# Two passes of a scan stage re-ordered: sums loaded by GpSimd, silu of the gate between differences and exponents, the inner norm's root ahead of splits

## The reference, cut to what matters

```python
cs = cumsum(dt * a)                                  # per head and chunk
lmat = exp(where(causal, cs[l] - cs[s], -inf))       # decay between two tokens of a chunk
cb = einsum('bclgn,bcsgn->bcgls', C, B)
y_diag = einsum('bcgls,bcgrls,bcsgrp->bclgrp', cb, lmat, x * dt)
states = einsum('bclgn,bclgr,bclgrp->bcgrpn', B, exp(cs[-1] - cs), x * dt)
# scan over chunks: h = exp(cs[-1]) * h + states
y_off = einsum('bclgn,bcgrpn,bclgr->bclgrp', C, h_before, exp(cs))
g = (y_diag + y_off + d * x) * silu(z)
out = (g * rsqrt(mean(g * g over the group) + 1e-6) * w) @ w_ssd_branch
```

## Time and profile before

| | |
|---|---|
| median of three runs | 2505.2 us |
| the profiled execution | 2507.65 us |
| its span, first to last instruction | 2505.8 us |
| mean granted clock | 0.989 |
| TensorE matmuls busy | 2414.6 us, 96% |
| VectorE busy | 1546.3 us, 62% |
| ScalarE busy | 873.8 us, 35% |
| GpSimd busy | 60.2 us, 2% |
| round 13, pass 1, first transposes | 1413.99 |
| second half of tile 21, pass 1, start | 1500.43 |

### The profile page before, as it was taken

The page is one execution under the profiler, slowest core; times in us unless marked ns, Lnnn a source line. Parts: engine busy times, 40 slices in busy tenths (PEclk is TensorE's granted clock), DMA queues, the critical chain, the costliest instruction groups (busy, mean ns, idle before and its releaser), DMA issues.

```text
span 2505.8 us, 38112 instructions
## 1 busy us (share of the span) xinstructions
PE 2414.6 (96%) x14805; PEld 2126.1 (85%) x14805; DVE 1546.3 (62%) x2792; ACT 873.8 (35%) x1343; POOL 60.2 (2%) x55
## 2 busy tenths in 40 slices
PE   6999999999989999999999899999998999999997
PEld 4888888888889988888879889888988899998996
DVE  5556344356479855444468876876665655883784
ACT  3123222134355532212245752763332333222122
POOL 0000000000112000000000000000100000000000
PEclk9999999999999999999999999999999999999999
DMA  4236223324443112222224422432211222223223
GB/s 146 88 97 145 100 101 125 128 84 129 139 114 77 35 51 90 95 101 84 100 84 113 109 68 86 115 90 83 86 67 64 82 73 80 101 84 134 85 88 114
DMA packets 90675, 240.34 MB, mean 96 GB/s; under 512 B 24818, under 2 KB 58098, under 8 KB 66546
## 3 DMA queue, kind: packets, MB, share of 16 engines
q1 hardware_dynamic: 29056, 198.26, 22.5%
q10 hardware_dynamic: 59716, 34.32, 6.3%
q0 software_dynamic: 1760, 5.77, 1.0%
HBM read 228.41 MB, written 10.09 MB: 95 GB/s over the span
## 4 chain that ended last, share of the span: by engine, by line
PE 87%; DVE 6%; issue 4%; ACT 2%; DMA 1%; ACTq 0%; DVEq 0%; POOL 0%
PE ps L984 42%; PE ps L1271 24%; PE ps L1524 4%; PE ps L1372 3%; PE ps L1225 3%; PE ps L1128 2%; PE ps L1206 1%; DVE wlo L1541 1%; PE ps L1457 1%; PE ps L1431 1%; DMA buckets<-in_buckets 1%; ACT L L829 1%; PE ps L1077 1%; PE ps L1004 1%; PE ps L999 0%
## 5 line engine op out<-in xcount | busy, mean ns | idle before, releaser
L527 ACT ACTIVATE whi<-raw 128x2048 fp32r<-128x2048 f32 x187 | 357.6, 1912 | 724.7 <-PE ps L984 472.7
L1541 DVE TENSOR_TENSOR wlo<-raw,whi 128x2048 fp32r<-128x2048 f32 (+1 forms) x208 | 430.7, 2071 | 72.7 <-ACT whi L527 72.1
L984 PE MATMUL ps<-parts,whi 128*128 128x512 f32 x1360 | 429.0, 397 | 0.0
L1271 PE MATMUL ps<-parts,whi 128*128 128x264 f32 (+1 forms) x2400 | 409.7, 293 | 11.3 <-DVE sq L2197 5.5
L1271 PEld LDWEIGHTS ps<-parts,whi 128*128 128x128 f32 x2400 | 334.7, 190 | 23.5 <-issue 17.8
L984 PEld LDWEIGHTS ps<-parts,whi 128*128 128x128 f32 x1360 | 255.2, 188 | 61.7 <-issue 1.6
L984 PE MATMUL ps<-parts,wlo 128*128 128x512 f32 x680 | 268.8, 395 | 0.0
L1271 PE MATMUL ps<-parts,wlo 128*128 128x264 f32 (+1 forms) x1200 | 243.8, 285 | 0.0
L984 PE MATMUL ps<-Mhi,whi 128*128 128x512 f32 x512 | 203.0, 396 | 0.0
L984 PE MATMUL ps<-Mlo,whi 128*128 128x512 f32 x512 | 203.0, 396 | 0.0
L984 PE MATMUL ps<-Mhi,wlo 128*128 128x512 f32 x512 | 203.0, 396 | 0.0
(11 more groups left out here) (373 smaller groups left out, 3888.3 us busy)
## 6 DMA issues: line engine op xcount, KB each, us to landing
raw<-in_stream SPq DMA_DIRECT2D x187, 1024.0 KB, 4.8
csb<-sums_d ACTq DMA_DIRECT2D x16, 512.0 KB, 5.8
bands<-scratch ACTq DMA_DIRECT2D x7, 1024.0 KB
near<-bands ACTq DMA_DIRECT2D x16, 256.0 KB, 2.6
csf<-sums_d ACTq DMA_DIRECT2D x32, 128.0 KB, 5.9
tabs<-bands ACTq DMA_DIRECT2D x8, 418.0 KB, 4.1
X<-in_x SPq DMA_DIRECT2D x4, 512.0 KB, 16.0
Q_odd<-parts POOLq DMA_DIRECT2D x8, 256.0 KB, 5.3
```

Source lines behind the costliest of these rows:

```text
L527: nc.scalar.activation(whi[:, s, :], raw[:, s, :], ACT.Copy).then_inc(hi_done, 1)
L984: mm = nc.tensor.matmul(out, w[:, s, at], x(k), start=k + j == 0, stop=k == k_tiles - 1 and j == 2)
L1271: mm = nc.tensor.matmul(ps[:, 2 * par + h, 0:w], wt[:, s, at], x[:, k, a + h * w:a + (h + 1) * w], start=k + j == 0, stop=k == k_tiles - 1 ...
L1541: low = nc.vector.tensor_tensor(wlo[:, s, a:b], raw[:, s, a:b], whi[:, s, a:b].bitcast(F32), ALU.subtract)
```

## The change

Five edits, all in the loop of the stage. `load_sums` goes from ScalarE to GpSimd, which issues the first two loads at the start of a pass and that of chunk n + 2 at the head of scan round n, ahead of its wait for the state. ScalarE's `decays` is cut in two, `differences` (the Relus) and `decays` (the exponents); from round 13 on the silu of z stands between them. The root of group 0's inner norm moves to the start of ScalarE's round 18, ahead of the weight copy, with its table loaded early by a dummy root; its variance moves to the head of VectorE's round 18, and `group_spread(0)` and the `Gv` copies from round 18 to 19. VectorE evacuates a tile ahead of `xdd`, which becomes `decayed_inputs`. The last square and variance of group 1 move ahead of round 20's split.

```diff
--- before.py
+++ after.py
@@ -497,8 +497,27 @@
             pool.wait_ge(lo_done, U0["half"] + 2)
             nc.gpsimd.memset(YS[:, :, :], 0.0).then_inc(ys_zero, 1)
             with pool.Fori(0, 2) as i:
+                def load_sums(n):
+
+                    gg, c = divmod(n, NC)
+                    at, w = CHUNKS[c]
+                    at += gg * (SSD_HPG * TOK)
+                    pool.dma_start(csb[0:w, n % 2, :, 0:w], bass.AP(sums_d.tensor, i * (2 * SSD_HPG * TOK) + at, [[0, w], [TOK, SSD_HPG], [1, w]])).then_inc(cs_loaded[n % 2], 16)
+                    for b in range(2):
+                        pool.dma_start(csf[b * DH:(b + 1) * DH, n % 2, :, 0:w],
+                                       bass.AP(sums_d.tensor, i * (2 * SSD_HPG * TOK) + (at + b * TOK), [[0, DH], [2 * TOK, SSD_HPG // 2], [1, w]])).then_inc(cs_loaded[n % 2], 16)
+
+                pool.wait_ge(cs_stored, 16 * NC)
+                pool.wait_ge(tok_diff, i + 1)
+                load_sums(0)
+                load_sums(1)
                 for r in range(1, 29):
                     gg, c = SCAN_AT.get(r, (0, NC))
+                    if c < NC and gg * NC + c + 2 < 2 * NC:
+                        pool.wait_ge(l_ready, i * 10 + (gg * NC + c + 1))
+                        if c:
+                            pool.wait_ge(ecs_ready, i * 8 + (4 * gg + c))
+                        load_sums(gg * NC + c + 2)
                     if c < NC - 2:
                         pool.wait_ge(h_new, i * 8 + (4 * gg + c + 1))
                         if gg + c == 0:
@@ -810,17 +829,7 @@
 
             own = Link(act, act_own)
             with own.loop(2, 10) as i:
-                def load_sums(n):
-
-                    gg, c = divmod(n, NC)
-                    at, w = CHUNKS[c]
-                    at += gg * (SSD_HPG * TOK)
-                    act.dma_start(csb[0:w, n % 2, :, 0:w], bass.AP(sums_d.tensor, i * (2 * SSD_HPG * TOK) + at, [[0, w], [TOK, SSD_HPG], [1, w]])).then_inc(cs_loaded[n % 2], 16)
-                    for b in range(2):
-                        act.dma_start(csf[b * DH:(b + 1) * DH, n % 2, :, 0:w],
-                                      bass.AP(sums_d.tensor, i * (2 * SSD_HPG * TOK) + (at + b * TOK), [[0, DH], [2 * TOK, SSD_HPG // 2], [1, w]])).then_inc(cs_loaded[n % 2], 16)
-
-                def decays(n):
+                def differences(n):
 
                     gg, c = divmod(n, NC)
                     w = CHUNKS[c][1]
@@ -829,27 +838,29 @@
                         relu = nc.scalar.activation(L[0:w, n % 2, h, 0:w], csb[0:w, n % 2, h, 0:w], ACT.Relu, scale=-1.0,
                                                     bias=tokh[0:w, CS, c, gg * SSD_HPG + h:gg * SSD_HPG + h + 1])
                     own.mark(relu)
+
+                def decays(n):
+
+                    gg, c = divmod(n, NC)
+                    w = CHUNKS[c][1]
                     if c:
                         if n >= 2:
                             act.wait_ge(y_done, i * 10 + (n - 1))
                         nc.scalar.activation(ecs[:, n % 2, :, 0:w], csf[:, n % 2, :, 0:w], ACT.Exp).then_inc(ecs_ready, 1)
                     own.wait()
                     nc.scalar.activation(L[0:w, n % 2, :, 0:w], L[0:w, n % 2, :, 0:w], ACT.Exp, scale=-1.0).then_inc(l_ready, 1)
-                    if n + 2 < 2 * NC:
-                        if c:
-                            act.wait_ge(ecs_ready, i * 8 + (4 * gg + c))
-                        load_sums(n + 2)
 
                 for r in range(29):
+                    if r == 18:
+                        nc.scalar.activation(spare[:, :], vec("eps"), ACT.Sqrt)
+                        act.wait_ge(gvar, i * 2 + 1)
+                        nc.scalar.activation(gtok[:, 0, 1, :], gtok[:, 0, 0, :], ACT.Sqrt).then_inc(gsqrt, 1)
                     if r and r % 2 == 0:
                         next_unit("half", r // 2 - 1, turn=i * 14, half_turn=i * 7)
                     if r == TOK_AT + 3:
                         act.wait_ge(tok_diff, i + 1)
                         nc.scalar.activation(tokh[:, DECAY, :, :], tokh[:, DECAY, :, :], ACT.Exp)
                         nc.scalar.activation(tokh[:, CDEC, :, :], ps[:, 5, 0:NC * SSD_HEADS // 2].rearrange("p (c h) -> p c h", c=NC), ACT.Exp).then_inc(tokh_ready, 1)
-                        act.wait_ge(cs_stored, 16 * NC)
-                        load_sums(0)
-                        load_sums(1)
                     if r in SCAN_AT:
                         gg, c = SCAN_AT[r]
                         n, w = gg * NC + c, CHUNKS[c][1]
@@ -857,21 +868,23 @@
                         if c < NC - 1:
                             nc.scalar.activation(Btok[0:w, :], ps[0:w, 5, 0:P], ACT.Copy).then_inc(btok_ready, 1)
                         if n + 1 < 2 * NC:
-                            decays(n + 1)
+                            differences(n + 1)
+                            if r < 12:
+                                decays(n + 1)
                     if 0 < r <= 12:
                         act.wait_ge(xbc_new, i * 12 + r)
                         nc.scalar.activation(conv_out(r - 1), conv_out(r - 1), ACT.Silu).then_inc(xs_ready, 1)
                         if r == TOK_AT + 4:
                             act.wait_ge(tokh_ready, i + 1)
+                            differences(0)
                             decays(0)
                     elif 12 < r <= 20:
                         q = r - 13
                         z = stg[:, q % 2, SSD_TAPS - 1:]
                         act.wait_ge(mt_free, i * 28 + (T0["half"] + r))
                         nc.scalar.activation(z, z, ACT.Silu).then_inc(z_silu, 1)
-                        if r == 18:
-                            act.wait_ge(gvar, i * 2 + 1)
-                            nc.scalar.activation(gtok[:, 0, 1, :], gtok[:, 0, 0, :], ACT.Sqrt).then_inc(gsqrt, 1)
+                        if r in SCAN_AT and n + 1 < 2 * NC:
+                            decays(n + 1)
                         act.wait_ge(z_new, i * 8 + (q + 1))
                         if q >= 2:
                             act.wait_ge(z_add, i * 8 + (q - 1))
@@ -883,8 +896,8 @@
                     if r == 20:
                         act.wait_ge(gvar, i * 2 + 2)
                         nc.scalar.activation(gtok[:, 1, 1, :], gtok[:, 1, 0, :], ACT.Sqrt).then_inc(gsqrt, 1)
-                    if r == 18 or r == 20:
-                        gg = (r - 18) // 2
+                    if r == 19 or r == 20:
+                        gg = r - 19
                         act.wait_ge(gspread, i * 2 + (gg + 1))
                         nc.scalar.activation(Gv[:, gg, N_META:], ps[:, 4 + 2 * gg, :], ACT.Copy)
                         nc.scalar.activation(Gv[:, gg, 0:N_META], ps[:, 5 + 2 * gg, 0:N_META], ACT.Copy).then_inc(grstd, 1)
@@ -1384,7 +1397,7 @@
                         row_tile(r, low)
                         scanned(*SCAN_AT[r])
                         row_tile(r, high)
-                    elif r == 18:
+                    elif r == 19:
                         row_tile(r, low)
                         group_spread(0)
                         row_tile(r, high)
@@ -2053,6 +2066,12 @@
                     own.wait()
                     l = L[0:w, n % 2, :, 0:w]
                     nc.vector.tensor_tensor(l, l, cbm[0:w, 0:w].unsqueeze(1).to_broadcast([w, SSD_HPG, w]), ALU.mult).then_inc(decayed, 1)
+
+                def decayed_inputs(gg, c):
+
+                    n, w = gg * NC + c, CHUNKS[c][1]
+                    by_head = lambda kind: tokh[0:w, kind, c, gg * SSD_HPG:(gg + 1) * SSD_HPG].unsqueeze(2).to_broadcast([w, SSD_HPG, DH])
+                    own.wait()
                     if c < NC - 1:
                         nc.vector.tensor_tensor(heads(xdd, w), heads(xdt, w), by_head(DECAY), ALU.mult).then_inc(xd_ready, 1)
 
@@ -2113,10 +2132,14 @@
                     nc.vector.scalar_tensor_tensor(YNlo[:, q, :], Y[:, q, :], gain_vec(q), YNhi[:, q, :].bitcast(F32), ALU.mult, ALU.subtract).then_inc(yn_ready, 1)
 
                 for r in range(21):
+                    if r == 18:
+                        group_variance(0)
                     if r in SCAN_AT:
                         turned(*SCAN_AT[r])
                     if r:
                         evacuate(r - 1)
+                    if r in SCAN_AT:
+                        decayed_inputs(*SCAN_AT[r])
                     if r % 2 and 8 < r < 18:
                         split_low("half", r // 2 - 1, i * 14, 1)
                     if r == TOK_AT + 1:
@@ -2125,8 +2148,6 @@
                         last_sums()
                     if r >= 14:
                         add_square(r - 14)
-                    if r == 18:
-                        group_variance(0)
                     if 0 < r <= 12:
                         convolve(r - 1)
                     if r in SCAN_AT:
@@ -2137,10 +2158,11 @@
                         group_root(0)
                     for q in range(*((0, 7) if r == 19 else (7, 8) if r == 20 else (0, 0))):
```

(5 more changed lines are left out.)

## The result

The changed kernel takes 2491.09 us (median of 4 runs, 2489.32 to 2493.43), the kernel before 2506.05 beside it (4 runs, 2503.77 to 2511.22). The ratio is 0.9937, with a 95% interval of 0.9924 to 0.9949: faster by 15.0 us, where 15.7 were forecast. The profiled spans are 2490.1 and 2505.8.

A forecast was written before the change was run, and what follows sets the result against it. TensorE, busy 96% of the span, was taken as the bound, with idle and low-clock time to win. Gains of 7.4 (pass 1) and 8.3 (pass 2) sum to 15.7: 2505.2 - 15.7 = 2489.5 us, range 2483 to 2501 for 8 in 10.

The forecast's parts named there:

- The windows: TensorE from round 13 to the second half of round 21, each pass: 79.0 us forecast, against 86.44 and 87.33.
- Length times (1 - clock): Rule for TensorE time lost at low clock in the windows: 4.5 us in pass 1, 5.0 in pass 2.
- The new waits: TensorE in rounds 20 and 21: tile 19's evacuation 1.75 us, z's last low part 1.35, group 1's Gr 2.05.
- Gr's and the clock's terms: Tail of each pass: a new wait of 2.05 us for Gr, plus 1.5 for low clock, between nothing and 3.3.
- VectorE ends Hs 0.4 to 0.7 before TensorE wants it: Scan rounds laid out after the silu move: VectorE keeps that margin in us, 10.0 from gate to gate with splits.
- One of the signs of being wrong: ScalarE's Relus waiting for a DMA; the others: a csb issue over 5 us, or L's product waiting for ScalarE.
- It costs from issues of about 8.5 on: GpSimd's loads: issuing costs time only from about 8.5 us a load (12.3 + 2 - 5.8).
- Rival (a): GpSimd becomes the bound in scan rounds, issues stretched to 13.3 us: 48 us lost, 2537 in all; chance 0.08.
- The 6.5 for Hs stays: Rounds 8 to 11: VectorE remains the bound with unchanged work, so TensorE's 6.5 us wait for Hs remains.
- (b): Gain eaten by late loads in rounds 14 to 16 or VectorE's missed margin: 4.7 us left, 2500.5; chance 0.14.
- (c): Tail better than laid out, no clock fall and low parts sooner: 20.7 us gained, 2484.5; chance 0.13.
- (d): Silu order changes nothing, VectorE waiting for the evacuated tile; only the root's 5.6 us less new waits, about 2505; chance 0.04.

The follow-up runs named there:

- silu_only: The kernel before with only z's silu put between Relus and exponents on ScalarE, loads left there: median 2498.33 us, ratio 0.9958 to the kernel before.
- root_only: The kernel before with only group 0's root and variance ahead, and group 1's last square and variance ahead of the split: 2506.71 us, ratio 0.9996.
- act_loads: The changed kernel with the loads of the sums back on ScalarE, behind L's exponents: 2493.85 us, ratio 0.9942 to the kernel before.
- evac_late: The changed kernel with xdd ahead of the evacuation again, as in the kernel before: 2494.45 us, ratio 0.9949 to the kernel before.
- tail: The changed kernel with VectorE's and ScalarE's order in rounds 20 and 21 rewritten, tile 19 evacuated among the low parts: 2484.22 us, ratio 0.9907.
- issues10: The changed kernel with each GpSimd load issued as ten DMAs, csb head by head: 2498.39 us, ratio 0.9964 to the kernel before.
- hd_psum: The changed kernel with GpSimd's Hd a round later, beside VectorE's PSUM reads instead of its split: 2493.74 us, ratio 0.9948 to the kernel before.

## Why the prediction was right

*Direction, size and cause* hold. The sum was 15.7, the medians differ by 15.0, and the profiled spans by 15.7. That the last two agree so closely is partly luck: the windows gained 2.1 more than the sum, and 2.1 were lost elsewhere. The parts stand where they were put: silu ahead of the exponents removes the stalls for L (silu_only), the root's order those for Gr and the sums (root_only), GpSimd's loads add nothing to them (act_loads). The root's part is shown by its waits and windows; its share of the median is not, since alone it gave no difference.

*The windows* were forecast at 79.0 = 71.6 work + 5.9 idle + 1.5 clock, and are 78.1 = 72.2 + 4.3 + 1.6.
- The work at full clock was 0.6 short: 72.16 in evac_late and tail, against 71.6. "Length times (1 - clock)" took 4.5 off the 76.10 of the earlier trace rows, and 3.9 had been lost. Why the product overstates it by a seventh stays open.
- The new waits: tile 19 1.46 (1.75 forecast), low part 1.06 (1.35), Gr 0.51 (2.05), spread 0.76 (0.76). The first three lie where they were laid out, each smaller than forecast.
- Gr's and the clock's terms are where the sum was off most. The text put the low clock between nothing, "most is covered by the wait of 2.05", and 3.3, and then summed 1.5 of clock and all of 2.05 of wait. In the changed kernel it is 1.6 + 0.51, in evac_late 0 + 1.83: about 2, not 3.55. Where the clock falls behind the wait instead (act_loads, pass 1), it is 1.83 and some 2.9 more, outside the window. So the two may be paid together, but in no run as 1.5 and 2.05 within it.
- A wait of 0.47 for L wasn't foreseen. "VectorE ends Hs 0.4 to 0.7 before TensorE wants it" left out that Hd would meet the split: VectorE took 10.7 from gate to gate (1434.64 to 1445.38), not 10.0, because the half split took 2.07. The earlier trace rows had shown the price to GpSimd (1.96 against 1.04), and the text applied it to GpSimd alone.

*What the windows gained above the span.* 17.8 against 15.7. Round 13 of pass 1 started 3.1 later than before (1417.10, 1413.99), and 1.0 came back behind the last window. Over the versions with three DMAs a load that start lies anywhere from 1410.82 (act_loads) to 1417.10. Ahead of the windows the clock falls in other places from one profiled kernel to the next; the forecast had no term for that. What sets these places stays open.

*The loads.* 2.2 a load, not 3, and no cost, as said. One of the signs of being wrong did show, once and small: at 1590.82 ScalarE's Relus waited 0.46 for csf, the third load of pass 2, and TensorE did not wait for L behind it. The start of a pass is where issues10 loses its time too. "It costs from issues of about 8.5 on" was wrong on both sides of it: at 5.9 they cost 6 to 7 us, because the two first loads are issued back to back, which the rule (made for a load in mid-pass) did not see; at 8.7, where it gives next to nothing, they cost 16, because Hd and a load fill the round. Rival (a) stood on csb issues stretched far beyond the 1.06 that was the longest here. GpSimd's issues of csb took 0.57 to 1.06 while VectorE was busy for 32.81 of the 35 us from 1380 to 1415, and the one at 1436.19, beside the split of 2.07, took 0.94. The Trainium skill's rule that VectorE can lock GpSimd out of writing descriptors (DMA: Bandwidth & Descriptors, SWDGE vs HWDGE vs iDMA) is stated there for VectorE's two-port mode, a condition that the prediction left out; no run here shows that mode, and the rule had no price here.

*The evacuation.* "The 6.5 for Hs stays": it became 6.0, and 6.5 again in evac_late. The swap is worth 0.5 outside the windows and nothing in them.

*Rivals.* (b) didn't come: loads are never late in rounds 14 to 16, and of VectorE's margins one in each pass was missed, by 0.47. (c) didn't come by itself; tail shows that the waits of the tail had to be ordered away, and then its gain of 20.7 is passed (a ratio of 0.9907 is 23). (d) is refuted by silu_only; root_only, which is close to the case that (d) describes, comes out at no change, as (d) priced it.

## What to carry to other kernels

Move the instruction that the bottleneck's supplier waits for, not those around it: the silu order alone gave two thirds of the gain, and the moved loads, which relieve the same engine, nothing on top. When a stall goes, lay out what is late next in the same order of instructions; these waits are as real as the removed one, and here re-ordering the tail gave 7.5 us more. A low clock that runs into a wait is not to be added to it in full; one that comes behind the wait is (2.5 to 3.3 us in three runs here). A queue's slack has to be read at the start of a loop too, where two of its jobs stand in line.

## What the runs showed of the hardware

A tensor operation of GpSimd stretches one of VectorE as well as the other way round. In round 14 the gate (0.70) held back Hd (1.44 for 1.04), and Hd then the half split (2.07 for 1.22); the delays, 0.40 and 0.85, are about what was left of the instruction that ran first. The Trainium skill states this (SBUF — State Buffer, SBUF: two separate sides): the one that starts first keeps the shared port pair for its whole instruction. With Hd beside reads of PSUM (hd_psum) both took their plain time, and eight of the twelve Hd of that run took 1.04 or 1.05, where the changed kernel's have a median of 1.436.

The same bytes make far fewer packets from GpSimd's queue. The queues of the page, before and then after (packets, MB, share):

```profile
q10 hardware_dynamic: 59716, 34.32, 6.3%
q0 software_dynamic: 1760, 5.77, 1.0%
```

```profile
q0 software_dynamic: 5984, 18.52, 4.0%
q10 hardware_dynamic: 31620, 21.57, 3.6%
```

12.75 MB moved in 28096 packets from ScalarE's queue (59716 - 31620) and in 4224 from GpSimd's (5984 - 1760), with nearly the same time to landing, 5.8 and 6.0.

An issue of GpSimd depends on its runs, but weakly: 0.57 with 128 runs (csb of a pass's first chunk, 16 partitions of eight runs) and 0.94 with 1024, so, as an estimate from these two, 0.0004 us a run, not the 0.0046 of the prediction's upper bound.
